# Layer 2 of a two-layer block: biases of the value projection as rounded parts, and the further expert blocks placed before the last eight experts

## The reference

```python
p_in = h @ w_in + b_in                       # layer 2, columns v, tq, tk, tv: 1216 of them
...
scores = sigmoid(h @ w_router)
_, idx = top_k(scores + b_router, 8)         # eight experts for each token
wts = scores[idx] / sum(scores[idx]) * 2.5
yb = swiglu(h_pad[tok], w_e_gate[e], w_e_up[e], w_e_down[e]) * wt[:, None]
return acc.at[tok].add(yb)                   # sum over the eight experts of a token
...
x = x + g_ffn * y                            # then the last rms_norm
```

## Time and profile before

| what | us |
|---|---|
| median of 3 runs | 2021.46 (2020.92 to 2022.41) |
| time of the profiled execution | 2019.52 |
| its span, first to last instruction | 2017.4 |
| PE busy | 1851.0 (92%) |
| DVE busy | 868.7 (43%) |
| ACT busy | 544.8 (27%) |
| POOL busy | 463.5 (23%) |
| last expert's down product ends | 1903.8 |
| last further block's down product ends | 1958.5 |
| first of the 16 row loads is issued | 1962.9 |

### The profile page before, as it was taken

One profiled execution on the slowest core, in us unless ns is written; L12 is line 12 of the kernel. 1 busy time (PEld: TensorE's weight loads), 2 busy tenths in 40 slices (PEclk: granted clock), 3 DMA queues, 4 the chain that ended last, 5 costly groups with the idle time before them and its releaser, 6 DMA issues.

```text
span 2017.4 us, 32223 instructions
## 1 busy us (share of the span) xinstructions
PE 1851.0 (92%) x13126; PEld 1246.2 (62%) x13127; DVE 868.7 (43%) x2029; ACT 544.8 (27%) x1037; POOL 463.5 (23%) x523
## 2 busy tenths in 40 slices
PE   6898999789888799999999999999999999999877
PEld 3677788644444588787666678456556555566432
DVE  3155644443221433624776324254544453444325
ACT  4142612411211342524676214011111111111102
POOL 1000000032221100011542000135444543454320
PEclk9998999989999899999999999989999999999998
DMA  9664631489999641154766143379999999999878
GB/s 388 240 244 170 240 133 63 174 325 418 417 416 410 234 163 64 63 114 104 151 140 130 64 177 126 139 297 406 395 369 412 409 412 376 411 393 401 336 277 353
DMA packets 103191, 532.31 MB, mean 264 GB/s; under 512 B 28082, under 2 KB 28386, under 8 KB 48380
## 3 DMA queue, kind: packets, MB, share of 16 engines
q1 hardware_dynamic: 64208, 457.73, 57.2%
q0 software_dynamic: 36256, 64.54, 11.6%
q10 hardware_dynamic: 2572, 7.81, 1.1%
HBM read 524.34 MB, written 51.90 MB: 286 GB/s over the span
## 4 chain that ended last, share of the span: by engine, by line
PE 74%; DMA 18%; DVE 4%; ACT 2%; issue 2%; SPq 0%; POOL 0%; POOLq 0%; DVEq 0%; ACTq 0%
PE ps L254 31%; PE ps L1766 18%; DMA arena<-in_egu 10%; PE ps L1840 9%; DMA arena<-in_ada 4%; PE ps L1735 3%; DMA arena<-y_rows 2%; PE ps L415 2%; PE ps L3164 1%; PE ps L1827 1%; DMA y_rows<-arena 1%; PE ps L2309 1%; PE ps L3190 1%; PE ps L1090 1%; PE ps L1096 1%
## 5 line engine op out<-in xcount | busy, mean ns | idle before, releaser
L1766 PE MATMUL ps<-arena 128*64 128x256 f32 x4096 | 480.3, 389 | 46.8 <-DMA arena<-in_egu 37.7
L1766 PEld LDWEIGHTS ps<-arena 128*64 128x64 f32 x4096 | 298.8, 140 | 246.1 <-issue 61.9
L254 PE MATMUL ps<-arena 128*128 128x256 f32 (+4 forms) x1268 | 313.8, 405 | 9.0 <-DVE arena L1298 3.8
L254 PEld LDWEIGHTS ps<-arena 128*128 128x128 f32 (+1 forms) x1268 | 215.2, 191 | 91.8 <-issue 67.4
L1723 POOL DMA_INDIRECT y_rows<-arena x160 | 165.0, 1031 | 392.8 <-DVE arena L1876 249.0
L1840 PE MATMUL ps<-arena 128*64 128x512 f32 x1024 | 242.4, 602 | 11.5 <-DVE arena L1835 4.0
L1717 POOL DMA_INDIRECT arena<-h_rows,arena x160 | 174.5, 1091 | 272.9 <-DVE arena L1709 119.0
L1814 ACT ACTIVATE arena<-ps 128x256 f32<-128x256 f32 (+1 forms) x96 | 33.5, 349 | 671.1 <-PE ps L1766 358.8
L1835 DVE COPY arena<-ps 128x256 f32<-128x256 f32 (+1 forms) x96 | 36.5, 380 | 369.5 <-PE ps L1827 324.8
L3128 POOL DMA_DIRECT2D arena<-in_nabias x160 | 85.5, 542 | 283.2 <-PE ps L3006 156.3
L1840 PEld LDWEIGHTS ps<-arena 128*64 128x64 f32 x1024 | 66.8, 136 | 106.4 <-issue 100.7
(11 more groups left out here) (441 smaller groups left out, 2648.2 us busy)
## 6 DMA issues: line engine op xcount, KB each, us to landing
arena<-in_egu SPq DMA_DIRECT2D x204, 1024.0 KB, 10.7
arena<-in_ed SPq DMA_DIRECT2D x102, 1024.0 KB, 7.5
arena<-in_ada SPq DMA_DIRECT2D x48, 1024.0 KB
arena<-in_win SPq DMA_DIRECT2D x37, 1024.0 KB, 10.5
arena<-y_rows SPq DMA_DIRECT2D x20, 1024.0 KB
arena<-in_nabias POOLq DMA_DIRECT2D x96, 128.0 KB, 5.5
arena<-in_wout SPq DMA_DIRECT2D x8, 1024.0 KB
h_rows<-arena ACTq DMA_DIRECT2D x8, 512.0 KB, 2.9
```

Of the source, the lines that this page charges most:

```text
L254: z = pe.matmul(o, l, r, start=start and i == 0, stop=stop and i == len(pairs) - 1, skip_group_check=check)
L1766: z = pe.matmul(b[64 * j:64 * j + 64, 256 * s:256 * s + 256], XV[:, c, 64 * h:64 * h + 64], wk(k)[:, j * 256:j * 256 + 256], start=k == 0, ...
```

## The change

It has four parts.

1. **Biases.** The biases of the 1216 columns are loaded into two more partitions (64 and 96) of a region that DVE has set to zero; ACT rounds them (twice), DVE subtracts the rounded from the full one, so that partition 64 holds the rounded and partition 96 the rest. The bias matmul becomes one fp32r product over partitions 64 to 127, most of them zero, with ones in the two rows.
2. **Place of the further blocks.** In layer 2 they run between expert 55 and expert 56 (`S` = 56). Their rows, masks and results have buffers of their own in `X`. The rows of the first two blocks are gathered at expert 52 (`F` = S - 3). SP issues the first six block loads, the loads of expert 56 and gate and up of 57, then the loads of the later turns, and then the rest of 57, 58 and 59 as the last turn gives up its slots.
3. **The wait in a block.** DVE works out row numbers without waiting for a scatter; the number that the scatter reads is copied at the end (`further_up`), after a wait for the scatter of the same buffer a turn earlier.
4. **The last sum.** The row loads are ordered by k first. Rows of k are loaded once experts up to 57, 59, 61 and 63 have been scattered. DVE adds into the base directly: all rows of k = 0 and k = 2 (16 additions) and one row of k = 3 for tiles 2 and 3; PE adds k = 1 and the others of k = 3. The finish is one DVE instruction for a tile (L3762 of the changed kernel), after the additions of the next tile.

```diff
@@ pe_tokm
                 if q == 1 and bias is not None:
-                    w.wait_ge(*l2.to("bin", 1))
-                    z = pe.matmul(o, ones[0:1, :], bias, start=False, stop=True, skip_group_check=True)
+                    w.wait_ge(*l2.to("bias lo"))
+                    z = pe.matmul(o, BIN_ONES, bias, start=False, stop=True, skip_group_check=True)
@@ new
+        BIN_PARTS, BIN_ONES, BIN_HI = BINR[64:128, 0:1216], BINR[64:128, 1216:1344], BINR[96:97, 1344:2560]
+        def dve_bias_ones(dve, w):
+            w.wait_ge(*fa.st.to("over"))
+            dve.memset(BINR[64:128, 0:1344].bitcast(F32), 0.0).then_inc(*l2.up("dve", "bias zero"))
+            w.wait_ge(*l2.to("bias zero"))
+            for i, p in enumerate((64, 96)):
+                dve.memset(BINR[p:p + 1, 1216:1344].bitcast(F32), 1.0).then_inc(*l2.up("dve", "bias ones", i))
+        def act_bias_hi(act, w):
+            w.wait_ge(*l2.to("bin", 3))
+            act.activation(BINR[64:65, 0:1216], BIN[64:65, 0:1216], ACT.Copy).then_inc(*l2.up("act", "bias hi", 0))
+            act.activation(BIN_HI, BIN[96:97, 0:1216], ACT.Copy).then_inc(*l2.up("act", "bias hi", 1))
+        def dve_bias_lo(dve, w):
+            w.wait_ge(*l2.to("bias hi", 1))
+            w.wait_ge(*l2.to("bias ones", 1))
+            dve.tensor_tensor(BINR[96:97, 0:1216], BIN[96:97, 0:1216], BIN_HI.bitcast(F32), ALU.subtract).then_inc(
+                *l2.up("dve", "bias lo"))
@@ dve_further (in the loop)
-                        dve.wait_ge(L.sem(f"yo{m}"), i * 16 + (16 * j + 16))
                         further_start(dve, x, m).then_inc(sv, 1)
...
                         dve.wait_ge(L.sem(f"yo{j}"), i * 16 + 16)
+                        further_up(dve, j).then_inc(sv, 1)
-                        further_result(dve, j).then_inc(sv, 1)
+                        further_result(dve, x, j).then_inc(sv, 1)
@@ sp_further_among (new)
+            n = 0 if book.counting else sp_further_first(sp, x, L, fw)
...
+            sp_expert(sp, w, x, x.S)
+            sp_expert(sp, w, x, x.S + 1, (0, 1))
+            if not book.counting:
+                sp_further_rest(sp, x, L, fw, n)
+            parts = [(x.S + 1, 2)] + [(x.S + 2, i) for i in range(3)] + [(x.S + 3, i) for i in range(3)]
+            for k, (e, i) in enumerate(parts):
+                if k < 6 and not book.counting:
+                    sp.wait_ge(L.sem("pe"), n * (2 * KP) + (KP * (k // 3) + (LG0, LG1, LD)[k % 3] + 1 + PRE - 2 * KP))
+                sp_expert(sp, w, x, e, (i,))
@@ sp_results
             w.wait_ge(*L.st.to("over"))
-            for t in range(t0, t1):
-                for k in range(x.K // 2):
-                    s = ring.turn(st, ("rows", t, k), ("acc", t, 2 * k + 1) if k < 2 else ("summed", t, k))
+            for k in range(x.K // 2):
+                done = x.V * (x.E - x.K + 2 * k + 2)
+                for u in range(done - NY, done):
+                    w.wait_ge(*x.st.to("yo", u))
+                for t in range(4):
+                    s = ring.turn(st, ("rows", t, k), ("summed", t, k) if k % 2 else ("acc", t, 2 * k + 1))
@@ pe_xb
-            pe_experts(pe, w, xb, fb)
+            pe_experts(pe, w, xb, fb, 0, xb.S)
             pe_further(pe, w, xb, fb)
+            pe_experts(pe, w, xb, fb, xb.S, xb.E)
@@ dve_xb
-            dve_experts(dve, w, xb, fb)
+            dve_experts(dve, w, xb, fb, 0, xb.S)
             dve_further(dve, w, xb, fb)
+            dve_experts(dve, w, xb, fb, xb.S, xb.E)
+            for k in (0, 2):
+                dve_result_rows(dve, w, xb, cb, k)
             for t in range(4):
...
+                if t >= 2:
+                    dve_result_row(dve, w, cb, t, 7, cb.to("acc", t, 5))
...
+                if t:
+                    dve_finish(dve, w, t - 1)
+            dve_finish(dve, w, 3)
@@ dve_finish
-            dve.tensor_scalar(x3[:, t, 0:512], TSUM[t % 2][:, 0:512], r, None, ALU.mult).then_inc(*cb.up("dve", "out", t, 0))
+            dve.scalar_tensor_tensor(x3[:, t, :], x3[:, t, :], r, FN, ALU.mult, ALU.mult).then_inc(*cb.up("dve", "out", t))
```

More of the change, by code:

```diff
@@ L2119, in pool_further_fetches @@
             w.wait_ge(*L.st.to("gi", 1))
[L2120 to L2121 removed]
+            if x.S == x.E:
+                for n in range(2):
+                    w.wait_ge(*x.st.to("xt", last_user(x, NX, n)))
+            else:
+                w.wait_ge(*cb.to("base", 3))
             if not book.counting:
@@ L2308, in pe_results @@
                         c = 1024 * i + 512 * half
-                        z = pe.matmul(bs[half].ap, ident, s.ap[:, c:c + 512], start=False, stop=k == last and i == 1)
-                    if k == last and half == 0:
-                        z.then_inc(*st.up("pe", "half", t))
-                z.then_inc(*st.up("pe", "summed", t, k))
-        xa = Experts("a", 32, 1, 2, m1v, M1, w1v, H1, a["egu1"], a["ed1"], Y1)
+                        z = pe.matmul(bs[t, half].ap, ident, s.ap[:, c:c + 512], start=i == 0, stop=False)
+                z.then_inc(*st.up("pe", "summed", t, 1))
+            for t in range(4):
+                s = ring.of(st, "rows", t, 3)
+                w.wait_ge(*s.landed)
+                for half in range(2):
+                    for i in range(2 if t < 2 else 1):
+                        c = 1024 * i + 512 * half
+                        z = pe.matmul(bs[t, half].ap, ident, s.ap[:, c:c + 512], start=False, stop=i == 1 or t >= 2)
+                    z.then_inc(*st.up("pe", *(("summed", t, 3) if half else ("half", t))))
+        xa = Experts("a", 32, 1, 2, 32, m1v, M1, w1v, H1, a["egu1"], a["ed1"], Y1)
         fa = Further(xa)
```

341 lines of the change are left out of this document (185 added, 156 removed).

## The result

The changed kernel takes 2001.68 us (median of 4 runs, 2000.37 to 2010.13), the kernel before, measured beside it, 2021.19. The ratio is 0.9917, with a 95% interval of 0.9898 to 0.9937: 17 us faster by the ratio (the two medians themselves stand 19.5 us apart), where 32 were forecast.

What follows compares the result with a forecast made beforehand. PE was taken to set the pace for most of the span, with a serial tail bound by row loads. Gains 13.5 + 0.65 + 18.3 = 32.4 us gave 1987.1 from the profiled execution, 1989 us against the median; range 1984 to 2000.

Steps and rivals of the forecast that it cites:

- Biases: Value projection: each bias product costs one 0.12 us beat like its neighbours, over 20 products a gain of 13.5 us.
- Rival A: Value projection: bias products don't overlap their neighbours, so 7 us gained instead of 13.5; 1995.5 us, chance 0.15.
- Place of the blocks: Layer 2 seams: the waits removed slightly outweigh those added by a second drain of the pipeline, net -0.65 us.
- Restarting expert 56: Seam behind the blocks: restarting this expert's gate costs between nothing and 1.83 us, taken as 0.9 us.
- Tail: From PE's last down product to the end: bound by DVE's program, 40.6 us instead of 58.9, a gain of 18.3 us.
- done in time for each tile: Tail: PE's 28 products with the identity take 26 us beside DVE's work and are ready for each tile.
- rival B: Tail: DMA engines, already busy among the experts, set the end; priced at 6 us, 1995 us, chance 0.2.
- B's sign: Tail: if DVE waits there for transfers, the rival that the DMA engines set the end is right.
- A and B together: Bias products not overlapping and DMA engines setting the end, most of both: 2001.5 us.
- D's mechanism: Tail: SP reaches its row loads only after the last down product, so some 3 us gained there; 2005 us, chance 0.05.
- C: Last eight experts: row loads crowd out scatters, so DVE and PE wait; about 2040 us, chance 0.03.

Runs made afterwards that it cites:

- e48: Not a run: a point in PE's timeline, the first gate product of expert 48 in layer 2; T is the end of PE's last down product.
- bias_128: Changed kernel with the bias product over all 128 rows of the array instead of rows 64 to 127, zeros elsewhere: 1998.15 us, ratio 0.9891.
- bias_only: Kernel before with only the changed bias products, copies and memsets; blocks and row loads as before: 2017.54 us, ratio 0.9985.
- rows_late: Changed kernel with SP's row loads held back until PE's last down product: 2016.78 us, ratio 0.9991.
- less_adds: Changed kernel with DVE's eight additions of k = 0 cut to 8 of 1024 elements: 2001.90 us, ratio 0.9917.
- after_again: Changed kernel, unaltered, run and profiled a second time: 2001.85 us, ratio 0.9916.
- after: First profile of the changed kernel, unaltered: profiled execution 2010.13 us, median 2001.68 us, ratio 0.9917.
- early_seam: Changed kernel with the further blocks between experts 53 and 54 instead of 55 and 56: 2005.22 us, ratio 0.9936.
- old_bias: Changed kernel with the plain fp32 bias products of the kernel before: 2011.07 us, ratio 0.9957.
- warm_tail: Changed kernel with 9 extra PE products ahead of the last tile's sum of k = 1: 1998.70 us, ratio 0.9907.
- best: Changed kernel with 128-row bias products, all k = 3 rows on PE, 5 extra products ahead of them, and short seam fills: 1989.01 us, ratio 0.9854.

## Why the prediction was wrong

The direction was right, and so was the place of the gains. All three terms were mis-sized, each to the favourable side, and the time came out 1.7 us above the range. By the stages, the gain is 6.05 (biases) less 4.4 (e48 to T: 204.6 on average over the four traces with the blocks behind expert 63, 209.0 over the nine with them ahead of expert 56, row loads beside the experts and no fill in the seam), plus 14.3 (tail), so 16 us, which the ratio shows as 17.

**Biases: 6.05 us instead of 13.5.** The step that failed is "I take 13.5, since nothing but its rows differs from its neighbours". Its rows were just what mattered: over all 128 of them the same product gives the 13.5 us (bias_128). Rival A, with its 7 us, had the mechanism and nearly the size. The row that spoke for it, 0.22 instead of 0.12 us after a bias, I had laid to the change between plain and rounded fp32; it stayed at 0.22 with rounded parts on 64 rows, and went with 128. The hidden parts (memsets, copies, subtraction) were rightly costed at nothing.

**Place of the blocks: +4.4 us instead of -0.65.** Three steps failed. "Removed: PE's 3.24 us wait for the first block's rows ... and the slow first gate product": of the wait only 0.7 us hung on the rows (bias_only), and the slow product is not tied to them but comes behind the pause of PE, which the new seam has too; 6.46 us instead of 5.25. "the first block waits for the result of expert 55 (1.41 us)": this wait is 2.56 us, of which 1.09 stand behind the result and have no row of their own. And the last down product, 1.96 us in the earlier trace rows, ran at half clock in the changed kernel's first trace (3.19). With 0.9 us less for expert 56 (below), 1.55 + 1.21 + 1.15 + 1.23 - 0.9 = 4.2 us of the 5.05 are accounted for; the rest stays open. Restarting expert 56, which I had put at 0.9, costs nothing: its gate stands 6.9 us behind the last block's, at the end of that block. The gathers ahead of the blocks did work: no PE wait for rows stands there.

**Tail: 44.9 and 44.2 us instead of 40.6.** The working by DVE's program was right where DVE works (additions 19.25 us, forecast 19.8; from the end of the additions to the end of the span 18.1 us without the waits, forecast 19.4). What failed is "done in time for each tile". I had let the last scatter land 3 to 8 us after its issue and each load follow in 2.6 us; the scatter took 7.0 and the first load 7.8 us, beside the other row loads, so that the first rows of k = 3 came at T + 18.7 and PE's products on them, at half clock, after DVE had run out of work. The end is then set by transfers, PE and DVE in turn.

That is rival B's mechanism in part. The DMA share is 1.02 at 421 GB/s from 1960 to 1980, and a load that I had counted at 2.6 us took 7.8. The Trainium skill says (DMA: Bandwidth & Descriptors, section "Issuing engines are not separate DMA queues") that transfers of all engines run on the same 16 DMA engines and interleave; the trace agrees, since the scatter that POOL issued took 7.0 us beside the row loads of SP, where the median among the blocks was 3.4. But B's sign, that DVE waits for transfers, didn't come: DVE waited for PE, and PE for the transfers. Its price of 6 us was above the 4.3 and 3.6 us by which the tails of the two traces exceed 40.6. A and B together, 2001.5 us, come within 0.2 us of the measured time by luck: the 5.05 us of the seams stand in neither, and the forecast with all three misses is 1989 + 7.45 + 5.05 + 4 = 2005.5 us, which are the 16 us of the stages against the kernel before. D's mechanism was tried in rows_late: it would have given 2017, not 2005. C didn't come: the blocks kept 8.3 us each in every trace (33.2 us for four), and DVE's waits from 1840 on, in the changed kernel's first trace, name PE and ACT and no scatter.

## What to carry to other kernels

A small operation put into a dense stream of matmuls should have the shape of its neighbours, all 128 rows included, even where most of the rows are zeros: here that is 7.35 us for 20 products. When work is moved ahead to hide transfers, price each new seam as a whole (its waits, also the part that no other engine explains, and the matmul clock behind the pause), and ask when the transfer that starts the last chain lands among all others, not how long one takes alone. An engine whose program is long isn't the bound until it is shown that it never waits: making it shorter (less_adds) tells it in one run.

## What the runs showed of the hardware

- A weight load of 64 rows (64 to 127) between loads of 128 rows isn't done beside the matmul before it: steps of 0.21 and 0.32 us instead of 0.12, and 0.22 behind; with 128 rows 0.12 throughout. The Trainium skill says (TensorE: Matmul & The Clock Gate, section "The mechanism") that loads overlap matmuls in flight only when they target other row groups, or go to the background weights. Here the loads of the same 128 rows overlap every time, so the first of these conditions isn't what lets them, and whether the second is, no run shows; the load of half the rows doesn't overlap.
- The granted clock fell to 0.5 (1.2 GHz; 0.50 from 1834 to 1840 and from 1974 to 1978 in after_again) behind pauses of PE of 2.6 us (seam) and 4.1 us (tail), and in some traces behind the one of 1.8 us before the last down product: 3.17 to 3.62 us for its eight records instead of 1.94 in after, after_again, bias_128 and early_seam, and 1.94 in less_adds, old_bias, rows_late and warm_tail. Behind the same pause of 2.6 us it fell in nine traces and not in two others. With 1.7 us of unused products in that pause it stood at 1.00 in the one trace that has them (best).
- A plain fp32 product of 128x512 is two records of 0.44 us: the 16 records of eight of them with the identity take 7.03 to 7.41 us.
